# Window attention of the sample tokens in four 32-column groups of the array, with every key and value load on the sync engine's queue

## The reference, cut to what matters

```python
def dilated_window_decode(q, k_all, v_all, slopes, window, dil):
    ...
    s = jnp.einsum('bthe,btkhe->bhtk', q.astype(F32), kg) * (Dh ** -0.5)
    s = s - slopes[:, None, None] * offs.astype(F32)[None, None, :]
    s = jnp.where(valid[None, None], s, -jnp.inf)
    lse = jax.nn.logsumexp(s, axis=-1)
    p = jnp.exp(s - lse[..., None])
    o = jnp.einsum('bhtk,btkhe->bthe', p, vg)
    return o, lse.transpose(0, 2, 1)

# per batch: 4 new tokens, 8 heads of 64, a cache of 2048 keys, patterns (128,1), (512,4), (2048,16)
parts = [dilated_window_decode(qa, k_all, v_all, slopes, w, d) for (w, d) in A_PATTERNS]
o_a = combine_patterns(parts).reshape(B, S, A_WIDTH)
```

## Time and profile before

| | us |
|---|---|
| median of three runs (3420.22 to 3422.05) | 3420.89 |
| profiled execution, time | 3423.01 |
| profiled execution, span of the trace | 3421.3 |
| PE busy over the span | 3128.2 (91%) |
| PE weight loads busy | 2773.2 (81%) |
| DVE / ACT / POOL busy | 1417.3 / 847.9 / 321.5 |
| granted TensorE clock, mean | 0.958 |

### The profile page before, as it was taken

One profiled execution on the slowest core, in us unless ns is written; L12 is line 12 of the kernel. 1 busy time (PEld: TensorE's weight loads), 2 busy tenths in 40 slices (PEclk: granted clock), 3 DMA queues, 4 the chain that ended last, 5 costly groups with the idle time before them and its releaser, 6 DMA issues. The chain is left out here.

```text
span 3421.3 us, 50617 instructions
## 1 busy us (share of the span) xinstructions
PE 3128.2 (91%) x20146; PEld 2773.2 (81%) x20146; DVE 1417.3 (41%) x2751; ACT 847.9 (25%) x1588; POOL 321.5 (9%) x313
## 2 busy tenths in 40 slices
PE   2999999698999999999888999978889999999997
PEld 2888899445999999999855666655688999999997
DVE  4244444333454444444422222233335544444445
ACT  3344312112222211211212223222323221121113
POOL 3111132110300000000100000022213000000001
PEclk6999999898999999999999999989989999999998
DMA  3221111551188921110001000045411211111101
GB/s 121 79 63 45 51 45 45 211 172 59 50 295 290 318 77 37 61 49 25 7 34 45 15 8 15 8 155 186 156 56 56 62 49 37 37 61 49 37 25 54
DMA packets 207706, 277.45 MB, mean 81 GB/s; under 512 B 16027, under 2 KB 179477, under 8 KB 202133
## 3 DMA queue, kind: packets, MB, share of 16 engines
q1 hardware_dynamic: 195032, 152.04, 14.4%
q0 software_dynamic: 12544, 123.61, 10.2%
HBM read 258.47 MB, written 84.07 MB: 100 GB/s over the span
## 5 line engine op out<-in xcount | busy, mean ns | idle before, releaser
L784 PE MATMUL psum<-mlp_halves,w_up 128*128 128x352 f32 x6336 | 1021.0, 323 | 17.1 <-DVE mlp_halves L514 13.7
L784 PEld LDWEIGHTS psum<-mlp_halves,w_up 128*128 128x128 f32 x6336 | 1016.0, 189 | 19.7 <-DVE mlp_halves L514 14.8
L822 PE MATMUL psum<-acts,w_down 128*128 128x352 f32 x3168 | 514.9, 323 | 7.8 <-DVE xT L965 6.4
L822 PEld LDWEIGHTS psum<-acts,w_down 128*128 128x128 f32 x3168 | 508.9, 188 | 10.4 <-DVE xT L965 7.6
L1407 PE MATMUL psum<-h_ab,w_in_halves 128*128 128x352 f32 x2016 | 341.9, 327 | 38.1 <-POOL w_in_halves L1707 37.1
L965 DVE TENSOR_TENSOR xT<-xT,psum 128x352 f32<-128x352 f32 x528 | 274.5, 520 | 237.1 <-PE psum L822 237.1
L1407 PEld LDWEIGHTS psum<-h_ab,w_in_halves 128*128 128x128 f32 x2016 | 323.2, 189 | 52.4 <-POOL w_in_halves L1707 37.6
L871 ACT CAST acts<-window 128x1056 fp32r<-128x1056 f32 x44 | 47.4, 1077 | 706.7 <-PE psum L822 572.3
L461 POOL TENSOR_TENSOR norm_temps<-norm_temps 128x352 f32<-128x352 f32 x72 | 76.4, 1073 | 1447.4 <-ACT norm_temps L452 1444.6
L585 PE MATMUL psum<-mlp_halves,project_w 128*128 128x352 f32 x1152 | 189.8, 328 | 15.1 <-DVE project_w L613 15.1
L585 PEld LDWEIGHTS psum<-mlp_halves,project_w 128*128 128x128 f32 x1152 | 188.5, 192 | 15.8 <-DVE project_w L613 15.3
(11 more groups left out here) (323 smaller groups left out, 3576.9 us busy)
## 6 DMA issues: line engine op xcount, KB each, us to landing
mlp_raw<-in_w_up SPq DMA_DIRECT2D x88, 512.0 KB, 5.1
out_new_a_k_s<-in_cache_a_k POOLq DMA_DIRECT2D x8, 4088.0 KB, 15.5
out_new_a_v_s<-in_cache_a_v POOLq DMA_DIRECT2D x8, 4088.0 KB, 15.2
mlp_raw<-in_w_down SPq DMA_DIRECT2D x22, 1024.0 KB, 6.2
w_in_raw<-in_w_in_ab SPq DMA_DIRECT2D x28, 512.0 KB, 4.6
ws_k_rows<-in_cache_a_k SPq DMA_DIRECT2D x8, 1024.0 KB, 8.0
ws_v_rows<-in_cache_a_v POOLq DMA_DIRECT2D x8, 1024.0 KB, 8.2
ws_k_rows<-in_cache_a_k SPq DMA_DIRECT2D x24, 256.0 KB, 3.5
```

Source lines behind the costliest of these rows:

```text
L784: mm = nc.tensor.matmul(c.bank[TILES * part + n][:, 0:TILE], w_up[s][:, w, part, k, :], h[:, x, k, tokens_of(n)], start=k + w + x == 0, st ...
L822: mm = nc.tensor.matmul(c.bank[6 + t % 2][:, 0:TILE], w_down[:, w, s, o * P:(o + 1) * P], acts[s][:, x, tokens_of(n)], start=s + w + x == ...
```

## The change

`window_samples` becomes the class `WindowSamples`, with buffers at fixed addresses and its load semaphores made before `MixerAb`; this adds one `open` (semaphore increments on POOL and a barrier) ahead of the mixer.

- A batch's 32 queries are spread over four chunks of heads, two heads (8 columns of 32) in each. Chunk h's scores go to PSUM partitions 32h to 32h+31, from the 128 features of these two heads alone. The bias tables are 128 rows high. One DVE instruction negates, adds the bias and takes the minimum; ACT exponentiates 128 x 928 in place.
- `weigh` multiplies chunk h's probabilities by the 128 features of its heads only, at partitions 32h: 28 products of 128 columns and 4 for the new keys, for 7 of 512 and one. One product turns the result.
- Keys turned for batch b go to one of two `kT` buffers, through three PSUM banks rather than four.
- All loads are issued by SP in the order of use. Tables, keys and values of batches 0 and 1 (`first_rows`) are issued in the mixer, ahead of the last head's two stores, once the projection has ended. In the stage: values of batch 2, then keys and values of b = 2 to 7. Values have three buffers.
- The output projection's first two weight loads are issued at the stage's end (`early`), ahead of the reading back of `xT`.

```diff
+                        if hd == B_HEADS - 1:
+                            sp.wait_ge(projected, START + TILES * CHUNKS)
+                            samples.first_rows(sp)
                         sp.wait_ge(state_ready, START + QB * (hd + 1))
                         sp.dma_start(d["new_ret_p"][0, 0, hd], state[:, QB, :]).then_inc(ret_stored, 16)
...
+    def first_rows(self, sp):
+        d = self.c.d
+        for dst, name in ((self.bias[0][:, 0:self.PAST], "past_bias"), (self.bias[1][:, 0:self.PAST], "past_bias"),
+                          (self.new_bias[:], "new_bias"), (self.own_head[:], "own_head"), (self.pick[:], "pick_step")):
+            sp.dma_start(dst, d[name]).then_inc(self.tables_in, 16)
+        for b in range(self.K_RING):
+            self.load(sp, "k", b)
+            self.load(sp, "v", b)
...
+                self.load(sp, "v", 2)
+                for b in range(self.K_RING, DEC_BATCH):
+                    sp.wait_ge(k_turned, START + key_unit(b - self.K_RING, G - 1) + 1)
+                    self.load(sp, "k", b)
+                    if b >= self.V_RING:
+                        sp.wait_ge(valued, START + b - self.V_RING + 1)
+                        self.load(sp, "v", b)
+                project.early(sp, w_out)
                 sp.dma_start(c.xT[:], c.spill).then_inc(c.restored, 16)
...
+                    for lo, hi in ((0, 512), (512, PAST)):
+                        for h in range(HC):
+                            nc.tensor.matmul(scores[rows_of_chunk(h), lo:hi], queries[:, h, b, :], kT[b % 2][:, h, lo:hi], start=True, stop=True)
+                    for h in range(HC):
+                        mm = nc.tensor.matmul(scores[rows_of_chunk(h), PAST:KEYS], queries[:, h, b, :], k_sample[:, h, :], start=True, stop=True)
...
+                    for g in range(G):
+                        for h in range(HC):
+                            nc.tensor.matmul(c.bank[OUT][rows_of_chunk(h), 0:P], probs_T[:, g, rows_of_chunk(h)], v_rows[b % self.V_RING][:, g, h * P:(h + 1) * P],
+                                             start=g == 0, stop=False)
...
+                for b in range(DEC_BATCH + 2):
+                    if b < DEC_BATCH:
+                        turn_keys(b, range(0, 3))
+                    if b >= 2:
+                        spread_out(b - 2)
+                    if b < DEC_BATCH:
+                        turn_keys(b, range(3, G))
+                    if 1 <= b <= DEC_BATCH:
+                        turn_probs(b - 1)
+                    if b < DEC_BATCH:
+                        score(b)
+                    if 1 <= b <= DEC_BATCH:
+                        weigh(b - 1)
...
+                        nc.vector.tensor_tensor_reduce(probs[:], scores[:, 0:KEYS], bias[b % 2][:], -1.0, 3e38, ALU.add, ALU.min,
+                                                       neg_max[:, b:b + 1]).then_inc(biased, 1)
```

More of the change, by code:

```diff
@@ L86, in tables, with by_chunk @@
     sl = slopes[np.arange(32) // DEC_SEQ][:, None]
-    out["past_bias"] = (log_count(d) - sl * np.maximum(d, 0)).astype(f)
+    def by_chunk(a):
+        full = np.zeros((A_HEADS // 2, 32) + a.shape[1:], f)
+        full[:, 0:8] = a.reshape((A_HEADS // 2, 8) + a.shape[1:])
+        return full.reshape((P,) + a.shape[1:])
+    out["past_bias"] = by_chunk(log_count(d) - sl * np.maximum(d, 0))
     tok = np.arange(SAMPLES)
@@ L90, in tables @@
     own = (tok // DEC_SEQ)[None, None, :] == np.arange(DEC_BATCH)[None, :, None]
-    out["new_bias"] = np.where(own, log_count(d) - sl[:, :, None] * np.maximum(d, 0), MASKED).astype(f)
+    out["new_bias"] = by_chunk(np.where(own, log_count(d) - sl[:, :, None] * np.maximum(d, 0), MASKED))
     causal = np.full((P, DEC_BATCH, SAMPLES), MASKED)
@@ L146, in __init__ @@
         self.bank = [psum[:, i, :] for i in range(8)]
-        self.scores = [psum[:, 2 * s:2 * s + 2, :].rearrange("p b n -> p (b n)") for s in range(2)]
+        self.scores = [psum[:, 2 * s:2 * s + 2, :].rearrange("p b n -> p (b n)") for s in range(3)]
         self.xT = self.tile("xT", [P, KC, TOKENS])
@@ L712, in rest_up, with __call__ @@
                                        ALU.subtract).then_inc(self.up_split, 1)
-    def __call__(self, layer, w_out, mix, gain, project, norm, restored, beside=None):
+    def __call__(self, layer, w_out, mix, gain, project, norm, restored, begun, beside=None):
         self.prepare(layer)
@@ L737, in __call__ @@
         next_sums = norm.sum_up(temps[1][:], True)
-        project.begin(w_out, mix, h, project_raw, project_weights, sums)
+        project.begin(w_out, mix, h, project_weights, sums)
         if True:
@@ L1934, in window_samples @@
     OLD, RECENT = 3, 4
-    PAST = (OLD + RECENT) * P
+    GROUPS = OLD + RECENT
+    PAST = GROUPS * P
     KEYS = PAST + SAMPLES
[L1937 to L1945, removed]
@@ L1960, in window_samples @@
[L1960 to L1980, removed]
-        new_v = v_sample[0:SAMPLES].rearrange("p a n -> p (a n)")
-        def load(eng, rows, x, b, s, signal):
-            old = caches[x][bass.ds(b, 1), 0:A_BUF - 512].rearrange("a (m r) n -> m (a r) n", r=16)
-            recent = caches[x][bass.ds(b, 1), A_BUF - 512:A_BUF].rearrange("a (k p) n -> p (a k) n", p=P)
-            for g in range(OLD):
-                eng.dma_start(rows[s][:, g, :], old[32 * g:32 * g + 32, 0:DEC_SEQ, :]).then_inc(signal[s], 16)
-            eng.dma_start(rows[s][:, OLD:, :], recent).then_inc(signal[s], 16)
@@ new lines, in load @@
+    def load(self, eng, x, b):
+        ring, rows, signal = (self.K_RING, self.k_rows, self.k_in) if x == "k" else (self.V_RING, self.v_rows, self.v_in)
+        s = b % ring
+        old = self.caches[x][b, 0:A_BUF - 512].rearrange("(m r) n -> m r n", r=16)
+        recent = self.caches[x][b, A_BUF - 512:A_BUF].rearrange("(k p) n -> p k n", p=P)
+        for g in range(self.OLD):
+            eng.dma_start(rows[s][:, g, :], old[32 * g:32 * g + 32, 0:DEC_SEQ, :]).then_inc(signal[s], 16)
+        eng.dma_start(rows[s][:, self.OLD:, :], recent).then_inc(signal[s], 16)
```

321 lines of the change are left out of this document (165 added, 156 removed).

## The result

The changed kernel takes 3315.74 us (median of four runs, 3312.86 to 3319.02) against 3421.47 for the kernel before beside it (3420.22 to 3426.11), a ratio of 0.969 with an interval of 0.967 to 0.971. That is 105.7 us less where 96 were forecast. The profiled run took 3318.41, its span 3316.9. The second leaves out the jitter of what comes ahead (the last matmuls of the mixer's projection begin anywhere between 596 and 599 us). That piece was 820.88 - 602.60 = 218.3 us and is now 714.88 - 601.37 = 113.5.

What follows compares the result with a forecast made beforehand. PE was taken to bound the stage, then DMA. The projection's first matmul moves from 820.9 to 724.3, 96.6 us less; 0.9 for the added open leaves net -95.7, so 3325 us; range 3308 to 3347, own range 3314 to 3338.

Steps and rivals of the forecast that it cites:

- the opening: Stage start: the mixer's last store lands behind 8.46 MB of loads at about 634, so the stage opens at 636.7 us.
- The rate of the loads: Key and value loads in the stage: 311 GB/s, 5.9 us a load, 11.8 us a batch; bounds 415 and 229.
- a batch on PE: PE's work per batch in the stage: 9.5 us, for 19.62 before.
- The tail: Stage's end, after the last batch is scored: bias and maximum to writing `mix`, 8.5 us.
- The projection's start: From the stage's last write at 719.5 to the output projection's first matmul at 724.3: 1.15 + 3.7 us.
- The open ahead of the mixer: A barrier added before the mixer: between 0 and 2.7 us, taken as 0.9.
- After the stage: Second projection and MLP: untouched; nothing outside 602 to 840 us moves by more than 2.
- (a): Rival, stage loads: 415 GB/s, faster than taken, PE binds, opening at 631, first matmul 717, kernel 3318 us; chance 0.08.
- (b): Rival, stage loads: the queue behaves like single loads, 229 GB/s, first matmul at 757, kernel 3358 us; chance 0.07.
- (e): Rival, loads in one queue so slow they use up the gain: from 152 GB/s; 3453 us at 130; chance 0.02.
- (c): Rival, PE products: weight loads don't overlap, 11.7 us a batch for 9.5, kernel 3338 us; chance 0.03.
- (d): Rival, scoring and weighing: column groups queue up, a batch is 18.7 us, kernel 3393 us; chance 0.03.

Runs made afterwards that it cites:

- one_group: Changed kernel with the products of all four chunks sent to PSUM partitions 0 to 31, one column group, each starting and ending its own sum; 3387.52 us.
- short_values: Changed kernel with loads of keys from batch 2 on and values from batch 3 on cut from 1.835 to 1.311 MB; 3310.09 us.
- store_between: Changed kernel with three loads ahead of the mixer's last stores, values 1 and 2 right behind them, nothing at the stage's opening; 3311.05 us.
- groups_alone: Changed kernel with keys on SP and values on POOL, both from the stage's opening as before, and no early weights; 3339.9 us.
- values_on_pool: Changed kernel with all loads of values issued by POOL at the same points, keys and tables by SP; 3320.45 us.
- changed_again: The changed kernel itself, unaltered, run again as partner of three other kernels on one chip; 3318.96 us.

## Why the prediction was right, and where its sizes were off

**The mechanism.** Four column groups run side by side, the transfers then set the pace, the store sets the opening: each was forecast, and each is shown above (one_group, short_values, store_between). Counted from the end of the mixer's projection the forecast for the first matmul was 724.3 - 602.6 = 121.7 us, and it is 113.5: 8.2 less, in three terms.

**The rate of the loads, 311 GB/s for 386.** This is the mis-sized term. The prediction read one row of 15 us and took it for the rate of full queues. In shorter stretches the same trace of before reads:

```profile
628.00:630.00 2.00, 0.00 (x0) 0.00 (x0) 0.00 (x0) 0.00 (x0) 2.00 (x4) 0.50 0.57 147
632.00:636.00 4.00, 0.00 (x0) 0.00 (x0) 0.00 (x0) 0.00 (x0) 0.94 (x2) 0.50 1.00 303
636.00:640.00 4.00, 0.00 (x0) 0.00 (x0) 0.00 (x0) 0.00 (x0) 0.00 (x0) 0.50 1.02 396
640.00:643.00 3.00, 0.00 (x0) 0.00 (x0) 0.00 (x0) 0.00 (x0) 0.00 (x0) 0.50 1.06 317
```

The first row is the start of the transfers. The prediction counted that start twice, once as "about 2 us after the issue" and once in the mean: without these 2 us the row's mean is (15 x 311 - 2 x 147) / 13 = 336. The others all have a full share and yet 303 to 396 GB/s. Short packets (the pieces in which the profile counts a transfer) suggest themselves as the reason. The answers on transfers for 630 to 636, 636 to 640 and 640 to 643, and for 656 to 692 of the changed kernel:

```profile
DMA packets 742, 1.84 MB, mean 306 GB/s; under 512 B 85, under 2 KB 85, under 8 KB 742
```

```profile
DMA packets 541, 1.59 MB, mean 396 GB/s; under 512 B 18, under 2 KB 18, under 8 KB 541
```

```profile
DMA packets 384, 0.95 MB, mean 317 GB/s; under 512 B 84, under 2 KB 105, under 8 KB 384
```

```profile
DMA packets 7235, 13.91 MB, mean 386 GB/s; under 512 B 476, under 2 KB 476, under 8 KB 7230
```

In these four, packets under 512 bytes are 11.5 and 22% of all at 306 and 317 GB/s, and 3 and 7% at 396 and 386. Other stretches break the pattern. In groups_alone, where both queues are full from the opening as in the kernel before, 631 to 635 and 643 to 647 read:

```profile
631.00:635.00 4.00, 0.00 (x0) 0.00 (x0) 0.00 (x0) 0.00 (x0) 2.35 (x6) 0.50 1.03 374
643.00:647.00 4.00, 1.16 (x6) 1.16 (x7) 0.00 (x0) 0.00 (x1) 0.00 (x0) 0.50 1.03 385
```

```profile
DMA packets 646, 1.50 MB, mean 374 GB/s; under 512 B 152, under 2 KB 156, under 8 KB 646
DMA packets 600, 1.54 MB, mean 385 GB/s; under 512 B 89, under 2 KB 89, under 8 KB 600
```

That is 374 GB/s with 24% of short packets and 385 with 15%; and in the kernel before, 634 to 636 has only 7% (15 of 222) at 287. So short packets don't explain the slow stretches, and why the kernel before was at 303 to 317 there stays open. What is shown is that keys and values flow at 386 from one queue (changed kernel), at 383 from two (values_on_pool), and at 374 and 385 from two full queues right after an opening (groups_alone). The early stretch of the changed kernel, with the tables in it, ran at 359.

This one term did two things. The 8.46 MB ahead of the store took 3.6 us less (8.46 MB at 359 for 311), so the opening came 631.68 - 601.37 = 30.3 us after the projection's end for 34.1 forecast, 3.8 less. And a pair of loads takes 9.5 us for 11.8, which let the batches run at PE's own pace up to batch 4. There the second term enters: **a batch on PE is 8.0 us, not 9.5.** Turning keys and the result took 3.5 together for 3.9, scoring 1.6 for 1.8, weighing 2.0 for 2.3, probabilities 1.0 for 1.1, and the allowance of 0.4 for changes of shape wasn't used. Both together bring the last write 710.51 - 631.7 = 78.8 us after the opening for 82.8 forecast, 4.0 less, the tail being 8.0 for 8.5. With PE at 8.0 the rate matters more than the prediction thought: it gave the transfers 1.7 us over PE at 311, and short_values shows 5 to 6 at 386.

**The projection's start** took 714.88 - 710.51 = 4.4 us for 4.85. In sum 3.8 + 4.0 + 0.5 = 8.3, which is the 8.2 of above but for rounding. From the first instruction of PE in the stage to the projection's it is 714.88 - 631.73 = 83.2 us for the 88 told beforehand.

**The open ahead of the mixer** was put at 0.9 us, a value chosen between bounds. It stands between the copies of the inputs and ACT's first instruction of the norm, in the kernel before and in the changed one:

```profile
33.62 2.43 ACT L452 ACTIVATE mix<-xT 128x352 f32<-128x352 f32 x6 [1.25 <-PEq L185]
33.15 2.43 ACT L460 ACTIVATE mix<-xT 128x352 f32<-128x352 f32 x6 [1.95 <-PEq L193]
```

ACT's wait grew from 1.25 to 1.95, 0.7 us (changed_again has 1.95 too). This is less than executions differ by: at the end of the mixer's projection the changed kernel was 1.2 us ahead of the one before.

**After the stage** nothing was to change. The gain was 106.0 us at the first matmul of the projection and 104.4 at the end. From that matmul to the end it is 2600.4 us in the kernel before, and 2602.0, 2602.9 and 2600.1 in the three profiles of the changed kernel, so the 1.6 us are within what its own executions differ by.

**How much of it was luck.** The forecast's own range, 3314 to 3338, came with two conditions: a rate of 280 to 380 GB/s and 9 to 10.5 us a batch on PE. Measured were 386 and 8.0, both outside and both to the fast side. The time, 3315.7, is inside that range by 1.7 us only.

**The rivals.** (a), with 0.08, was nearer in time than the forecast: 3318 for 3315.7 measured and 3325 forecast. It had the rate right in direction, though its reason, PE binding, was wrong: the transfers still set the pace. Its opening was added up wrongly: at 415 GB/s the 8.46 MB take 6.8 us less than at 311, which gives 636.7 - 6.8 = 629.9 and not 631, and a first matmul at 716 and not 717. Measured were an opening at 631.7, the last write at 710.5 and the first matmul at 714.9, each nearer to (a) than to the forecast. The evidence against it (2 KB rows at 311) was the row read too coarsely. (b) and (e) rested on rates of 229 and below that no full queue of these rows showed. (c) is refuted by the 56 weight loads in 1.47 us, (d) by one_group. PE started without a wait for keys, as forecast. The waits for keys of 1 to 2 us in the later batches came too, at 386 GB/s and not at 310. The two waits for copies in the first batches, 2.6 us together, the prediction did not have; it had named waits for copies rather than for keys as a sign of being wrong, and in the later batches none is left.

## What to carry to other kernels

Products that use 32 of 128 columns are worth laying into four column groups even when the number of instructions grows (16 instructions of 512 columns in 1.71 us for 6.20): count the time per set of four. Once that was done here the transfers were the next bound, and then the order in which every transfer is asked for is part of the critical path: a barrier waits for a small store behind 8.5 MB of loads as it does for work. To read a rate for a forecast, cut the row into stretches of a few microseconds, and leave the start of the transfers out of the mean where the sum counts it apart: that alone moves this one from 311 to 336. The rest of the way to 386 is not explained, so a range for the rate has to reach the fastest stretch that the trace shows.

## What the runs showed that was not expected

Loads on another queue hold up those that are needed first: the first keys were there 10.2 us after their issue when only tables were ahead of them, 18.9 when values came by another queue. With two queues the rate was 383 GB/s, with one 386. The Trainium skill (DMA: Bandwidth & Descriptors, section "Issuing engines are not separate DMA queues") says that initiating transfers from several engines saves only the time of issuing them. The two rates agree.

A mean share of 1.05 went with 386 GB/s and one of 1.00 with 303: the share alone does not tell the rate.

Weight loads of 32 columns were done at 1.47 us / 56 = 26 ns each while products of other column groups ran.
